# A fused two-block transformer kernel: a weight split moved out of the first expert unit's way, the last expert unit taken row by row, and the first tile's norms and gate products moved into the last two units

## What is computed

```
def peer_ffn(x, w_q, sub_keys, u_tab, v_tab):      # 8 heads, 16 experts per head and token
    qh = (xc @ w_q).reshape(Ct, H, 2, PEER_QDIM // 2)
    s = einsum("nhad,akd->nhak", qh, sub_keys)
    top_s, top_i = lax.top_k(s, K)                  # 16 best of 128 keys, twice
    best_s, pos = lax.top_k(cand, K)                # 16 best of their 256 sums
    gate = softmax(best_s)
    ug, vg = u_tab[eidx], v_tab[eidx]               # gathered rows of 1024 + 1024 numbers
    hpre = einsum("nd,nhkd->nhk", xc, ug)
    act = gate * gelu(hpre)
    return einsum("nhk,nhkd->nd", act, vg)
x = rms_norm(x + peer_ffn(rms_norm(x)), norm_final)
```

## Time and profile before

| | us |
|---|---|
| median of 3 runs | 2091.26 (2091.05 to 2093.32) |
| the profiled execution | 2100.45 |
| its span in the profile | 2098.4 |
| PE busy | 1892.0 (90%) |
| DVE busy | 1283.8 (61%) |
| ACT busy | 772.4 (37%) |
| POOL busy | 415.0 (20%) |
| gathers' queue, share of 16 engines | 31.5% |

### The profile page before, as it was taken

One profiled execution on the slowest core, in us unless ns is written; L12 is line 12 of the kernel. 1 busy time (PEld: TensorE's weight loads), 2 busy tenths in 40 slices (PEclk: granted clock), 3 DMA queues, 4 the chain that ended last, 5 costly groups with the idle time before them and its releaser, 6 DMA issues.

```text
span 2098.4 us, 31012 instructions
## 1 busy us (share of the span) xinstructions
PE 1892.0 (90%) x11358; PEld 1524.2 (73%) x11358; DVE 1283.8 (61%) x2521; ACT 772.4 (37%) x1288; POOL 415.0 (20%) x536
## 2 busy tenths in 40 slices
PE   7999999958778787887789999999999999879998
PEld 7999899823333333333369999999989999769997
DVE  4546855667777767777564556654565445666444
ACT  4346233222222122222134344444354334555333
POOL 4000000346554555555310000000000000110000
PEclk9989999978998998899999999999999999879999
DMA  8323266669999999999946564645546556415552
GB/s 235 98 80 116 67 172 190 251 251 421 422 421 421 422 421 422 422 422 422 422 155 213 186 200 151 201 154 191 186 154 205 193 180 200 141 32 165 185 181 99
DMA packets 231414, 496.72 MB, mean 237 GB/s; under 512 B 21653, under 2 KB 182566, under 8 KB 198566
## 3 DMA queue, kind: packets, MB, share of 16 engines
q1 hardware_dynamic: 188432, 221.36, 33.4%
q0 software_dynamic: 38224, 273.04, 31.5%
q10 hardware_dynamic: 4678, 1.21, 0.3%
HBM read 494.53 MB, written 1.05 MB: 236 GB/s over the span
## 4 chain that ended last, share of the span: by engine, by line
PE 67%; DMA 15%; DVE 8%; issue 5%; POOL 4%; ACT 2%; DVEq 0%; POOLq 0%; ACTq 0%
PE ps L2054 43%; PE acc L2054 23%; DMA rows_xl<-in_peer_uv,idx_now 12%; DMA arena<-in_peer_uv,idx_now 2%; POOL rows_lo L698 1%; POOL rows_xh L698 1%; DVE arena L1701 0%; DVE arena L1705 0%; DVE arena L1708 0%; POOL rstd L613 0%; DVE lo L1314 0%; DVE arena L2003 0%; POOL idx_now L693 0%; POOL arena L698 0%; DVE arena L1530 0%
## 5 line engine op out<-in xcount | busy, mean ns | idle before, releaser
L1314 DVE TENSOR_TENSOR lo<-raw,hi 128x2048 fp32r<-128x2048 f32 x198 | 451.6, 2283 | 311.7 <-ACT hi L753 311.6
L2054 PE MATMUL ps<-xh,hi 128*128 128x256 f32 x1896 | 540.8, 285 | 2.6 <-DVE xl L1335 2.1
L2054 PE MATMUL ps<-xl,hi 128*128 128x256 f32 x1896 | 538.4, 284 | 0.0
L2054 PE MATMUL ps<-xh,lo 128*128 128x256 f32 x1896 | 538.3, 284 | 0.0
L753 ACT ACTIVATE hi<-raw 128x2048 fp32r<-128x2048 f32 x198 | 376.6, 1905 | 276.0 <-PE ps L2054 230.8
L2054 PEld LDWEIGHTS ps<-xh,hi 128*128 128x128 f32 x1896 | 364.9, 192 | 6.0 <-issue 4.4
L2054 PEld LDWEIGHTS ps<-xl,hi 128*128 128x128 f32 x1896 | 365.1, 193 | 1.5
L2054 PEld LDWEIGHTS ps<-xh,lo 128*128 128x128 f32 x1896 | 364.9, 192 | 0.1
L608 POOL TENSOR_SCALAR ss<-ss 128x1 f32<-128x1 f32 x24 | 7.2, 298 | 1005.9 <-ACT arena L1132 879.1
L2054 PE MATMUL acc<-rows,diag 128*128 128x512 f32 x192 | 119.3, 787 | 92.0 <-ACT diag L1055 71.4
L2054 PE MATMUL acc<-arena,diag 128*128 128x512 f32 x384 | 178.7, 605 | 13.9 <-ACT diag L1055 13.9
(11 more groups left out here) (366 smaller groups left out, 3296.8 us busy)
## 6 DMA issues: line engine op xcount, KB each, us to landing
raw<-in_w_ffn_gate SPq DMA_DIRECT2D x44, 1024.0 KB, 5.3
raw<-in_w_ffn_down SPq DMA_DIRECT2D x44, 1024.0 KB, 4.9
raw<-in_w_ffn_up SPq DMA_DIRECT2D x40, 1024.0 KB, 5.4
raw<-in_w_in SPq DMA_DIRECT2D x29, 1024.0 KB, 5.3
raw<-in_w_conv_in SPq DMA_DIRECT2D x11, 1024.0 KB, 5.2
raw<-in_w_kv SPq DMA_DIRECT2D x6, 1024.0 KB, 5.3
raw<-in_w_out SPq DMA_DIRECT2D x4, 1024.0 KB, 5.2
arena<-in_w_ffn_up SPq DMA_DIRECT2D x4, 1024.0 KB, 7.9
```

Source lines behind the costliest of these rows:

```text
L1314: v.tensor_tensor(lo[s][:, 0:WORDS[p]], raw[s][:, 0:WORDS[p]], hi[s][:, 0:WORDS[p]].bitcast(F32), ALU.subtract).then_inc(lo_done, 1)
L2054: return nc.tensor.matmul(out, l, r, start=first, stop=last)
```

## The change

- ACT and DVE split ffn0's gate block between units 5 and 6 (DVE had done so after unit 0, ACT before it).
- In unit 0 DVE's order is now: dots 0, keys, dots 1, pairs, weigh 0, weigh 1, dots 2, index, weigh 2, dots 3, weigh 3.
- The buffers of rows 12 to 15 change places. Row 12 of unit 0 waits for less (`FIRST["peer_q"] + 1`), rows 13 to 15 wait as before. POOL loads norm_final's gain after unit 0's gathers, not after the last.
- Before unit 14 DVE adds tile 0's `ACC` to `x` and squares; in the middle of unit 14 it applies the final norm and squares again; in unit 15, after row 2, it scales `xn`. POOL's `norm_tile` steps of tile 0 stand in `gather` of unit 15.
- Unit 15 goes row by row on DVE, ACT and PE: dot, gelu, product, diagonal, two matmuls. PE transposes tile 0 after row 5, ACT and DVE turn it into `f0h` and `f0l` at rows 6 to 9 (these lie over the old scores), and PE makes tile 0's gate products, six at a time, after rows 10 to 13.
- After the stage only tile 1 is left. Its adds and scalings go by halves, its squares are ACT's (L1213). ACT and DVE copy `f0h` and `f0l` into `xh` and `xl` at the end.
- The spare block of ffn0 is loaded into `raw[late[1]]`, row 12's buffer, when the last row has landed and row 12 has been used. ACT splits it between the two pairs of squares. The second up panel, which uses the same buffer, is loaded after the spare block's split.
- POOL's clearing of tables after the stage waits until tile 1's `xn` is there.

The diff, cut to its core:

```diff
-        rows += [home[4], home[5], raw[late[0]][:, :], home[0]]
-        EARLY = 3
+        rows += [raw[late[1]][:, :], home[4], home[5], home[0]]
+        EARLY = 12
...
+                    dst = spare_raw
                 else:
-                    sp.wait_ge(v_used, UNITS * PE_K)
+                    sp.wait_ge(row_landed[PE_K - 1], 16 * UNITS)
+                    sp.wait_ge(v_used, UNITS * PE_K - (PE_K - 1 - EARLY))
+                    dst = raw[late[1]]
...
                     load(p0 + 1, column(gate, i), 3, i - 1)
+                    if f == 0 and isinstance(i, int):
+                        sp.wait_ge(spare_lo_done, s + 1)
                     load(p0 + 2, column(up, i), 3, i - 1)
...
+                        if isinstance(n, int) and n == 0 and k >= EARLY:
+                            pool.wait_ge(panel_used, FIRST["peer_q"] + 1 if k == EARLY else FIRST["ffn0"])
...
-            peeled(pool, UNITS, gather)
+            gather(0)
             load_gain("final")
-            for t in range(TT):
-                norm_tile("final", t)
-                norm_tile("f0", t)
+            with pool.Fori(1, UNITS - 1) as n:
+                gather(n)
+            norm_tile("final", 0)
+            gather(UNITS - 1)
+            norm_tile("final", 1)
+            norm_tile("f0", 1)
...
-            split(FIRST["ffn0"])
...
+            with act.Fori(1, PE_HEADS - 2) as n:
+                weights(n)
+                best_exp(n + 2)
+            split(FIRST["ffn0"])
+            with act.Fori(PE_HEADS - 2, UNITS - 2) as n:
...
+            for k in range(PE_K):
+                act.wait_ge(u_used, PE_K * n + k + 1)
+                nc.scalar.activation(pe_gelu[:, k:k + 1], pe_h[:, k:k + 1], ACT.Gelu).then_inc(gelu_done, 1)
+                act.wait_ge(act_ready, GROUPS * n + k + 1)
+                act.wait_ge(v_used, PE_K * n + k + 1 - DIAGS)
+                nc.scalar.activation(diag[:, k % DIAGS, :], ident[:, :], ACT.Copy, scale=pe_act[:, k:k + 1]).then_inc(diag_ready, 1)
+                if 6 <= k < 9:
+                    turn_tile("f0", 0, f0h, (k - 6,))
...
+            for b in range(HALVES):
+                square_half("final", b, 3 + b)
             split_spare(SPARE["ffn0"])
+            for b in range(HALVES):
+                square_half("f0", b, 5 + b)
+            turn_tile("f0", 1)
+            nc.scalar.activation(xh[:, :, 0:P], f0h.bitcast(F32), ACT.Copy).then_inc(f0_moved, 1)
...
+                if k == 5:
+                    turn_tile("f0", 0)
+                if k == 10:
+                    begin(FIRST["ffn0"])
+                if k in gate_ks:
+                    token_tile(FIRST["ffn0"], 0, bank(0)[:, 0:PC], lh=f0h, ll=f0l, ks=gate_ks[k], stream="f0")
```

More of the change, by code:

```diff
@@ L1062, in _, with turn_tile @@
             weights(UNITS - 2)
[L1063 to L1068 removed]
+            def turn_tile(name, t, out=xh, groups=range(len(TILE_KS))):
+                for g in groups:
+                    ks = TILE_KS[g]
                     if name in TURN_AT:
@@ L1769, in _ @@
             dve.wait_ge(q_rows, TT)
-            unit(0, 0, (0, 2))
-            split(FIRST["ffn0"])
+            gate(0)
+            dots(0, 0, 0)
+            best_keys(2, 0, 2)
+            dots(0, 0, 1)
+            best_pairs(2)
+            weigh(0, 0)
+            weigh(0, 1)
+            dots(0, 0, 2)
+            best_index(2)
+            weigh(0, 2)
+            dots(0, 0, 3)
+            weigh(0, 3)
             dve.wait_ge(pe_sc_ready, PE_HEADS - 1)
@@ L2459, in begin_spare @@
                 wait(pe, evacuated, EVAC[p])
+            n = UNITS - 1
+            gate_ks = {k: range(2 * (k - 10), 2 * (k - 10) + 2) for k in range(10, 14)}
+            for k in range(PE_K):
+                pe.wait_ge(diag_ready, PE_K * n + k + 1)
+                pe.wait_ge(row_landed[k], 16 * (n + 1))
+                for half in range(2):
+                    last = mm(ACC[:, 2 + half, :], diag[:, k % DIAGS, :], rows[k][:, D + half * 512:D + (half + 1) * 512], False, k == PE_K - 1)
+                    if k == PE_K - 1 and not half:
+                        last.then_inc(peer_half, 1)
+                last.then_inc(v_used, 1)
+                if k == 5:
[4 more added lines that the diff above has]
+                    token_tile(FIRST["ffn0"], 0, bank(0)[:, 0:PC], lh=f0h, ll=f0l, ks=gate_ks[k], stream="f0")
             def first_pair(stage, stream, lh=xh, ll=xl):
@@ L2466, in tile @@
                     return token_tile(None if w else p, t, bank(w)[:, t * PC:(t + 1) * PC], lh=lh, ll=ll, stream=stream)
+                if stage == "ffn0":
+                    turn_tile(stream, 1)
+                    tile(0, 1).then_inc(panel_used, 1)
+                    begin_spare(p, s)
+                    token_tile(None, 0, bank(1)[:, 0:PC], lh=f0h, ll=f0l, stream=stream)
+                    tile(1, 1).then_inc(spare_used, 1)
+                    pe.wait_ge(f0_moved, 2)
+                    return
                 for t in range(TT):
@@ L2475, in first_pair @@
                         last.then_inc(panel_used, 1)
-                    if stage != "ffn0":
-                        if not t:
-                            begin_spare(p, s)
-                        last = tile(1, t)
-                if stage == "ffn0":
-                    begin_spare(p, s)
-                    for t in range(TT):
-                        last = tile(1, t)
+                    if not t:
+                        begin_spare(p, s)
+                    last = tile(1, t)
                 last.then_inc(spare_used, 1)
```

111 lines of the change are left out of this document (76 added, 35 removed).

## The result

The changed kernel takes **2069.79 us** (median of 4 runs, 2067.32 to 2070.66), the kernel before beside it 2092.29 (4 runs, 2091.05 to 2096.93): ratio 0.9891, 95% interval 0.9877 to 0.9904. The forecast was 2060.7 with a range of 2057 to 2070. The direction and the mechanisms hold; the gain is 22.5 us where 30.6 were forecast, and those 8 us are the subject of what follows.

The account below looks back on a forecast made before the run. DMA transfers were taken to bound the expert stage, which could be shortened only at their pause or after the last of them. Terms of -19.8, -10.0 and -0.8 made -30.6 us: 2091.3 to 2060.7 us, range 2057 to 2070.

Parts of the forecast that it names:

- The pause goes: -19.8 us: Start of the expert stage: moving the gate block's split removes the 20.1 us transfer pause, saving 19.8 us; lower bound -7.
- the sum is in stages that transfers time, so I carry it over unscaled: Whole kernel: the -30.6 us read from the 2100.45 us profile is subtracted unscaled from the 2091.3 us median, giving 2060.7.
- the forecast's own bounds: Whole kernel: tail -9 to -12 and front -18 to -20.1 us give 2059 to 2064 us.
- Rival 1: Unit 0: PE runs at half clock, a further pause of 5 to 13 us, about 2069; chance 0.10.
- Rival 2: After the last dot: up block or second up panel comes late, +2 to +4 us, about 2064; chance 0.17.
- Tail, -10.0 us: End of the stage: from last dot's start to PE's up products 17.2 us instead of 27.2, saving 10.0 us.
- 0.75: Tail: DVE's scaling of tile 1 takes 0.75 us, not 1.34, with POOL's clearing behind it; otherwise the sum is -30.0.
- The clock back in the 96 products, -0.8, bounds 0 and -1.7: Up products after the stage: 96 products took 13.27 us against 11.5 at full clock; earlier PE work saves 0.8 us.
- The order of rows 12 to 15 ... into a queue that is full anyway: 0: Unit 0's gathers: one row goes some 12 us earlier into a full queue, worth 0 us.
- Rival 3: Last unit: PE at half clock takes 3.6 us a row against 2.485, piling up 18 us, about 2079; chance 0.04.
- Rival 4: Stage's start: the pause is set by something other than the split and returns; only 10.8 us remain, about 2080; chance 0.03.
- Rival 5: Whole stage: a lower granted clock makes PE the bound and the kernel slower, +103 against -31, about 2163; chance 0.02.

Follow-up runs that it names:

- first set: First four follow-up runs, on one chip: kernel before and changed kernel once more, and each half of the change alone; kernel before 2089.71 us, changed kernel 2071.20 us.
- first two profiles of the kernel before: Two profiled executions of the unchanged kernel before: the one the prediction used, 2100.45 us, and a repeat whose run timed 2091.37 us.
- the late row: The changed kernel with row 12 of unit 0 held back like rows 13 to 15: 2069.09 us, ratio 0.9886 to the kernel before.
- tail alone: The changed kernel with the gate block's splits and DVE's order in unit 0 as in the kernel before: 2089.28 us, ratio 0.9993.
- front alone: The kernel before with only the gate block's split behind unit 5 and DVE's new order in unit 0: 2084.27 us, ratio 0.9964.
- repeated profile of the changed kernel: The changed kernel, unchanged, profiled and timed once more: 2071.20 us, ratio 0.9904 to the kernel before.
- unit 1 row by row: The changed kernel with each gather of unit 1 issued when PE has done that one row, not four: 2069.62 us, ratio 0.9883.
- second and third profile of the kernel before: Two repeats of the kernel before, unchanged; their runs timed 2091.37 us and 2089.45 us.

## Why the prediction was right, and where it was off

- *"The pause goes: -19.8 us"*: **the step that was mis-sized.** The pause does go, and from profile to profile the last dot moved by 18.8 us. But an ordinary execution of the kernel before has 9.4 us of pause and its last dot at 1044.3 to 1045.1; the changed kernel's are at 1035.3 and 1037.9. The front is worth about 8 us (1044.7 - 1036.6). In the first set, where all profiles are of one kind, the trace adds up to the time: 7.2 us up to the last dot and 11.0 behind it make 18.2, and 18.5 were timed.
- *"the sum is in stages that transfers time, so I carry it over unscaled"*: this is how the error got into the number. The profiled execution stood 9.2 us above the median (2100.45 and 2091.26), and I took that as general slowness. It was for the most part the long pause itself, 20.1 against 9.4: of the 10.7 us between the spans of the first two profiles of the kernel before, 9.0 lie ahead of the last dot. From the profiled execution the text had worked out 2069.9. That 2069.79 was measured is a coincidence, for that sum belongs to the changed kernel's own profiled execution, which took 2067.32. It is luck too that the median lies in the stated range, 0.2 us inside: the forecast's own bounds were 2059 to 2064, and the range went on to 2070 for rivals 1 and 2, which are not what happened. When the profile lies well above the median, the stall that is being removed is the first suspect.
- *Tail, -10.0 us*: right in each step (17.17 against 17.2; 0.75; the up block not late), and a little more in the mean, since the old tail took 26.9 to 28.9 us in six profiles and the new one 17.2 to 17.6 in seven.
- *The clock back in the 96 products, -0.8, bounds 0 and -1.7*: 1.5 us in four of the six profiles with the old tail; in the other two the products took 11.8 us before the change too, but began 28.0 and 28.9 us after the last dot. Taken together, from the last dot to the span's end six profiles with the old tail give 1042.5 to 1045.1 us, mean 1043.7, seven with the new one 1030.3 to 1032.3, mean 1031.1: 12.6 us where the sum had 10.8. And 8 + 12.6 = 21 us lies between the 18.5 and 22.5 that were timed.
- *"The order of rows 12 to 15 ... into a queue that is full anyway: 0"*: true in the changed kernel, where the early and the late row give the same time. Alone it is the most harmful edit of all, +6.6 us in its own set, because "full anyway" was wrong: the queue thins out at 420, and the gate block lives on that. The change needed its two halves together: tail alone -0.4 us, front alone -5.4, both -18.5 to -22.5.
- *Rival 1, unit 0 at half clock*: it comes true in part. In the repeated profile of the changed kernel the clock reads 0.83 in 420 to 430, PE's first 12 products take 7.08 us instead of 5.39, and with POOL's two small operations (2.4 us instead of 0.6) the transfers have a dip of 2.4 us, not 5 to 13.
- *Rival 2*: the up block and second panel are not late, save once: with unit 1 row by row the panel's load took 8.4 us and PE waited 0.45 us. *Rival 3*: each of the last rows waits only for its transfer. *Rival 4*: falls with the windows. *Rival 5*: falls with the share of 1.00 or more up to 1025: the transfers bound every unit.

## What to carry to other kernels

Before a stall is booked at its full length, see it in two or three profiled executions, or at least ask whether the profile's distance from the median is that same stall. A load in small pieces that is issued into a queue of large ones gets packets and not bytes: its landing depends on when the other queue thins out, so an earlier prefetch elsewhere can delay it (here from 10.1 to 18.9 us after its issue), and a consumer should either not stand in front of the critical work or the other queue should be held for it. Measure the halves of a change also together: one that is worth nothing or harms alone may be harmless behind the other.

## What the runs showed of the hardware

- 1 KB packets of a direct load and 7.3 KB packets of gathers went in nearly equal numbers (853 and 893 in 18 us); nearly alone the direct load moved over 300 packets a us (608 and 653 in 2 us in the second and third profile of the kernel before).
- A transfer's last 4% can take as long as the rest: in the first profile of the kernel before 994 of 1040 packets went from 414 to 424, the other 46 in the 10 us after.
- Holding four gathers back until a blocking load was in cost nothing in the kernel before (2090.40 against 2090.56 us), and with the tail's edits brought the load in 8.8 us sooner.
- A clearing of 0.52 us on POOL that began 0.15 us ahead lengthened a DVE scaling from 0.75 to 1.28 us.
- In eight of fourteen profiles ACT begins a copy at 392 to 394 only after 3.6 to 3.7 us of idle, in six it does not; the cause is open.
